# Two groups of tiles instead of three in the first sequence's first feed-forward, own tokens for the small loads, later strip and convolution matmuls

## The reference

```
mod = silu(c) @ w_mod + b_mod                      # 9 vectors: shift, scale, gate x 3
x   = x + 0.5 * g1 * FFN1(mod(rmsnorm(x)))         # width 2816, SwiGLU; also for the context
p   = mod(rmsnorm(x)) @ w_in                       # q k v, output gate, decays, conv input, merge gates
o   = bidirectional chunked gated linear attention(q, k, v, decays), starts from the context's state
z   = GLU(conv input);  y = silu(layernorm(depthwise conv of width 31 (z))) @ w_conv_out
x   = x + g2 * ((sigmoid(ga) * y + sigmoid(gb) * gla_output(o)) @ w_out)
x   = x + 0.5 * g3 * FFN2(mod(rmsnorm(x)));  out = rmsnorm(x)
```

## Time and profile before

| | us |
|---|---|
| median of 3 runs | 7281.48 (7276.81 to 7284.88) |
| profiled execution, its own time | 7291.05 |
| its span on the slowest core (core 2) | 7289.4 |
| spans of the eight cores | 7261.0 to 7289.4 |
| first matmul of FFN1, sequence 0 | 116.09 |
| groups 2 and 3 of FFN1 begin | 408.51, 588.41 |
| phase B of sequence 0 | 763.67 to 1258.29 |
| phase B of sequence 1 | 2555.00 to 3002.12 |
| last cast issued | 1005.91 |

### The profile page before, as it was taken

The page is one execution under the profiler, slowest core; times in us unless marked ns, Lnnn a source line. Parts: engine busy times, 40 slices in busy tenths (PEclk is TensorE's granted clock), DMA queues, the critical chain, the costliest instruction groups (busy, mean ns, idle before and its releaser), DMA issues.

```text
span 7289.4 us, 111871 instructions; the slowest of 8 cores (7261.0 to 7289.4 us)
## 1 busy us (share of the span) xinstructions
PE 6791.2 (93%) x38936; PEld 3421.5 (47%) x38936; DVE 3072.9 (42%) x5068; ACT 2844.4 (39%) x4883; POOL 607.2 (8%) x570
## 2 busy tenths in 40 slices
PE   4989887999999998899999998899999999879999
PEld 1435544444454455344445455444445445534444
DVE  2232455543324255544333345554432435554432
ACT  2132555322314266433233346533332436643321
POOL 0000222000000022100000012110000002210000
PEclk7999988999999999899999999999999999989999
DMA  8898865555545445655554544645553654555554
GB/s 181 200 229 184 154 118 129 176 186 182 176 135 196 162 94 98 171 163 175 180 176 155 180 140 95 139 157 187 182 175 123 196 168 108 102 138 170 188 184 148
DMA packets 466131, 1166.10 MB, mean 160 GB/s; under 512 B 54192, under 2 KB 202160, under 8 KB 460144
## 3 DMA queue, kind: packets, MB, share of 16 engines
q1 hardware_dynamic: 461840, 1103.03, 51.0%
q0 software_dynamic: 3744, 55.91, 5.8%
HBM read 1097.14 MB, written 173.08 MB: 174 GB/s over the span
## 4 chain that ended last, share of the span: by engine, by line
PE 82%; DMA 10%; SPq 4%; DVE 2%; issue 2%; ACT 1%; POOL 0%; DVEq 0%; ACTq 0%; POOLq 0%
PE pb L594 82%; DMA ZS_b<-z_s 4%; SPq L591 4%; DMA WU_f<-w_mod 2%; DMA z_s<-ZR_b 1%; DMA WH_f<-w_mod 1%; DVE NM_f L620 1%; DMA x_s<-X_f 0%; DMA WR_d<-wdn_s 0%; DMA WM_f<-w_mod 0%; DMA WR_g<-wg_s 0%; DMA z_s<-NM_b 0%; ACT L613 0%; ACT NM_f L613 0%; DVE R_f L623 0%
## 5 line engine op out<-in xcount | busy, mean ns | idle before, releaser
L594 PE MATMUL pb<-uF_b,WR_g 128*128 128x512 bf16 x11264 | 2474.1, 380 | 20.4 <-DMA WR_g<-wg_s 15.7
L613 ACT ACTIVATE EV_f<-pb 128x512 f32<-128x512 f32 (+1 forms) x1322 | 766.0, 582 | 2554.0 <-PE pb L594 2517.1
L594 PEld LDWEIGHTS pb<-uF_b,WR_g 128*128 128x128 bf16 x11264 | 1103.1, 98 | 1346.2 <-issue 48.4
L594 PE MATMUL pb<-U2T,WR_g 128*128 128x512 bf16 x6272 | 1448.9, 384 | 24.2 <-ACT EV_f L613 21.5
L594 PE MATMUL pb<-hF_b,WR_d 128*128 128x512 bf16 x5456 | 1195.5, 380 | 9.1 <-DMA WR_d<-wdn_s 9.1
L620 DVE TENSOR_TENSOR hF_b<-EV_f,pb 128x512 bf16<-128x512 f32 x682 | 468.1, 687 | 1503.1 <-PE pb L594 1420.8
L594 PEld LDWEIGHTS pb<-U2T,WR_g 128*128 128x128 bf16 x6272 | 614.5, 99 | 730.0 <-issue 82.6
L594 PEld LDWEIGHTS pb<-hF_b,WR_d 128*128 128x128 bf16 x5456 | 534.5, 98 | 654.3 <-issue 23.5
L613 ACT ACTIVATE NM_f<-X_f 128x512 f32<-128x512 f32 x504 | 305.8, 625 | 1029.9 <-DVE X_f L623 927.0
L623 DVE SCALAR_TENSOR_TENSOR X_f<-pb,SC,X_f 128x512 f32<-128x512 f32 x384 | 284.3, 750 | 934.9 <-PE pb L594 934.6
L620 DVE TENSOR_TENSOR NM_f<-NM_f 128x512 f32<-128x512 f32 (+1 forms) x672 | 471.4, 715 | 64.7 <-ACT NM_f L613 40.3
(11 more groups left out here) (141 smaller groups left out, 5545.9 us busy)
## 6 DMA issues: line engine op xcount, KB each, us to landing
WR_g<-wg_s SPq DMA_DIRECT2D x1130, 512.0 KB, 4.0
WR_d<-wdn_s SPq DMA_DIRECT2D x496, 352.0 KB, 3.2
ZS_b<-z_s SPq DMA_DIRECT2D x512, 131.0 KB, 6.1
wg_s<-wg POOLq DMA_DIRECT2D x84, 512.0 KB, 10.9
X_f<-x SPq DMA_DIRECT2D x64, 512.0 KB, 7.9
x_s<-X_f SPq DMA_DIRECT2D x64, 512.0 KB, 8.2
X_f<-x_s SPq DMA_DIRECT2D x64, 512.0 KB, 8.1
out<-X_f SPq DMA_DIRECT2D x64, 512.0 KB, 5.1
```

Of the source, the lines that this page charges most:

```text
L594: return (lambda e: e.matmul(out, lhsT, rhs, start=start, stop=stop), reads, writes)
L613: [(lambda e: e.activation(out, in_, func, **kw), reads, writes)], FUNC_SETS.get(func, 0))
```

## The change

It has five parts.

1. **Groups.** In sequence 0 the feed-forward has two groups, tiles 3, 2 and the context, then tiles 1 and 0. The context gets buffers of its own there (HC0, UC0, XC0), for which WU goes from two buffers to one. Tiles 1 and 0 both go through UTX, and U2T is free once three users are done (`u2_part`).
2. **Tokens.** The small loads (cst, vecs, gn, wa, dwc) and the three paddings of z_s have a token each instead of one together; the paddings are written in a task of their own (`pads`) after the seventh block of the second group; the four WM strips are four tasks; the first group's x and context are loaded ahead of the third strip.
3. **Later by plan.** `dma(..., late=)` adds to the time at which the planner expects a transfer: 6 us for WU and WH strips, 3 us for the loads ZS_b, in all sequences.
4. **Casts.** FFN1's 38 casts are paced as before. The 16 of QK and V come over the second group, the 24 of the merge over phase B's 16 weight blocks, and the 30 of FFN2 one for each weight load after them. Before, the 40 of QK, V and merge came over groups 2 and 3, and the 30 of FFN2 two for each load of phase B.
5. **Priority.** `prep_c`, `mean_c` and `ln_chunk` of tile 0 get 2 instead of 5 in every sequence.

```diff
-                    op.fin = self.dma_free + 1.4
+                    op.fin = self.dma_free + 1.4 + sets
...
-        WMU = mkpool("WU", 2, {"f": ([128, 8, 512], F32, 0)}, 1, [u2off])
+        WMU = mkpool("WU", 1, {"f": ([128, 8, 512], F32, 0)}, 1, [u2off])
+        HC0 = mkpool("hC0", 1, {"b": ([128, NJ, NCX], BF16, 0)}, NJ, [u2off + 16384])
+        UC0 = mkpool("uC0", 1, {"b": ([128, 8, NCX], BF16, 0)}, 8, [end_ac])
+        XC0 = mkpool("XC0", 1, {"f": ([128, 8, NCX], F32, 0)}, 8, [SB_END - SB_END % 64 - 8192])
...
-        t_zpad = T()
+        t_zpad = [T() for _ in range(3)]
+        t_cst, t_vec, t_gn, t_wa, t_dw = T(), T(), T(), T(), T()
...
-                elif n < n_ffn + n_mid:
-                    tick = len(refs_ffn(0)) - 2 + (n - n_ffn) * (len(refs_a(0)) - len(refs_ffn(0))) // n_mid
+                elif n < n_b:
+                    tick = lf - 2 + (n - n_ffn) * (la - lf) // (n_b - n_ffn)
+                elif n < n_c:
+                    tick = la + (n - n_b) * 16 // 24 - 2
                 else:
-                    tick = len(refs_a(0)) + (n - n_ffn - n_mid) // 2
+                    tick = la + 16 + n - n_c
...
-                g = [xs[:2]] + [[t] for t in xs[2:]]
-                if len(g) > 1:
-                    g[-1].append(NTT)
-                else:
-                    g.append([NTT])
-                return g
+                return [xs[:2] + [NTT]] + [xs[n:n + 2] for n in range(2, NTT, 2)]
...
-                    yield dma("sp", 134144, zs.h["b"][16 * r:16 * r + 16, :, :], zsrc(blk, gi, r), reads=rd, writes=[zs.ts[r]], cost=0.65)
+                    yield dma("sp", 134144, zs.h["b"][16 * r:16 * r + 16, :, :], zsrc(blk, gi, r), reads=rd, writes=[zs.ts[r]], cost=0.65, late=3.0)
...
-            M.spawn(mean_c(s, i, cv), 0, 5)
+            M.spawn(mean_c(s, i, cv), 0, 2 if i == 0 else 5)
...
-                M.spawn(ln_chunk(s, i, c, cv, mean, va), 0, 5)
+                M.spawn(ln_chunk(s, i, c, cv, mean, va), 0, 2 if i == 0 else 5)
...
+                elif part == 2 and len(gr) > 1:
+                    yield wait("A", 0, gr[1][0], "h", (ch - 12) * 3)
...
+        def pads():
+            yield wait("A", 0, a_groups(0)[-1][0], "h", 6)
...
-            M.spawn(mod_task(range(0, 4), 0), 0, 0)
+            for ch in range(4):
+                M.spawn(mod_task([ch], 0), 0, ch // 2 * 2)
...
-            for dst, src in ((vecs[:], vecs_d), (gn[:], gn_d)):
-                yield dma("sp", 65536, dst, src, writes=[t_c])
+            yield dma("sp", 81920, vecs[:], vecs_d, writes=[t_vec])
+            yield dma("sp", 4096, gn[:], gn_d, writes=[t_gn])
...
-                M.spawn(prep_c(s, 0), 0, 5)
+                M.spawn(prep_c(s, 0), 0, 2)
```

More of the change, by code:

```diff
@@ L587, in build, with dma @@
         dsems = {e: [es.enter_context(nc.semaphore(f"d_{e}{i}")) for i in range(NDMASEM[e])] for e in ENGS}
-        def dma(q, nb, out, in_, reads=(), writes=(), cost=0.45, **kw):
+        def dma(q, nb, out, in_, reads=(), writes=(), cost=0.45, late=0, **kw):
             return ("op", q, cost if q != "pool" else 1.0,
-                    [(lambda e: e.dma_start(out=out, in_=in_, **kw), reads, writes)], nb, 0)
+                    [(lambda e: e.dma_start(out=out, in_=in_, **kw), reads, writes)], nb, late)
         def mmi(out, lhsT, rhs, start, stop, reads, writes):
@@ L778, in prep_a @@
             isx, W, col, tok0 = ainfo(s, ti)
-            late = (s, ti) == late_tile
+            late = (s, ti) in late_tiles
             if late:
                 yield wait("sc", 1)
-            X = yield acq(UTX if late else XP if isx else XCP)
+            X = yield acq(UTX if late else XP if isx else XCS[s])
             xf = X.h["f"]
@@ L785, in prep_a @@
             sm = yield from norm_sum(lambda c: xf[:, c, :W], X.ts, W)
+            if s == 0:
+                yield wait("const")
             rs = yield from rstd_of(sm, W)
@@ L800, in prep_a, with u2_part @@
                 M.flag("X", "A", s, ti)
+        def u2_part():
+            info["u2n"] = info.get("u2n", 0) + 1
+            if info["u2n"] == len(late_tiles) + 1:
+                u2_free()
         def u2_free():
             ops = []
-            for b in WMP.bufs[2:] + WMU.bufs + UTX.bufs:
+            for b in WMP.bufs[2:] + WMU.bufs + UTX.bufs + HC0.bufs:
                 ops += b.hist
@@ L848, in ffn @@
         def ffn(mem, which, after=None):
-            for (key, W, col, hb, up) in mem:
-                yield wait("u", *key)
             for j in range(NJ):
+                if j == 0:
+                    yield wait("u", *mem[0][0])
                 wb = yield from wnext(ref_g((G_GU1, G_GU2)[which] + j))
@@ L854, in ffn @@
                 for (key, W, col, hb, up) in mem:
+                    if j == 0:
+                        yield wait("u", *key)
                     u = info[key][1]
@@ L939, in phase_a @@
                 mem = []
-                hc = None
-                hp = None
+                extra = []
                 for n2, ti in enumerate(g):
                     isx, W, col, tok0 = ainfo(s, ti)
+                    hc = hb
                     if not isx:
-                        yield wait("u", "A", s, ti)
-                        hp = HCP
-                        hc = yield acq(hp)
+                        hp = HCS[s]
                     elif n2 == 1 and g[0] < NTT:
                         hp = HP2
+                    else:
+                        hp = None
+                    if hp is not None:
+                        if not isx and s > 0:
+                            yield wait("u", "A", s, ti)
                         hc = yield acq(hp)
-                    mem.append((("A", s, ti), W, col, hb if isx and hp is not HP2 else hc, UP if isx else UCP))
+                        extra.append((hp, hc))
+                    mem.append((("A", s, ti), W, col, hc, UP if isx else UCS[s]))
                 yield from ffn(mem, 0)
-                if hc is not None:
+                for hp, hc in extra:
                     hp.rel(hc)
-                if s == 0 and n == 0 and late_tile is None:
+                if s == 0 and n == 0:
                     yield wait("sc", 1)
-                    u2_free()
+                    u2_part()
                 for ti in g:
@@ L1026, in conv_task @@
                 zs = yield acq(ZS)
-                rd = [t_z[blk][i2] for i2 in near] + [t_zpad]
+                rd = [t_z[blk][i2] for i2 in near] + t_zpad
                 for r in range(8):
-                    yield dma("sp", 134144, zs.h["b"][16 * r:16 * r + 16, :, :], zsrc(blk, gi, r), reads=rd, writes=[zs.ts[r]], cost=0.65)
+                    yield dma("sp", 134144, zs.h["b"][16 * r:16 * r + 16, :, :], zsrc(blk, gi, r), reads=rd, writes=[zs.ts[r]], cost=0.65, late=3.0)
                 for e in range(2):
@@ L1054, in gates @@
         def gates(s, h, d, hl):
-            order = border[1:-1] + [border[0], border[-1]] if s == 0 and h == 0 else border
+            order = border
             pool = GD[d]
@@ L1622, in mod_task @@
                 PS.rel(pt)
-                if ch == 3:
-                    M.flag("sc", 0)
+                if ch < 4:
+                    info["sc0"] = info.get("sc0", 0) + 1
+                    if info["sc0"] == 4:
+                        M.flag("sc", 0)
                 elif ch == 5:
```

57 lines of the change are left out of this document (31 added, 26 removed).

## The result

The changed kernel takes 0.9863 of the time of before, 95% interval 0.9834 to 0.9892: some 100 us less than 7281 us. Two of its six executions, 7174.4 us (the profiled one) and 7188.4 us, ran with a granted clock of 0.97 or 0.98 on all cores; in the others the four cores of one half of the chip, or all eight, had a lower one and took 7866 to 8357 us, and such executions and cores are left out in all that follows. Over the eight cores of the profiled executions the median span fell from 7272.7 to 7160.4 us, 112 us. The forecast was 157 us.

What follows compares the result with a forecast made beforehand. PE, busy 93% of 7289.4 us, was taken as the bound, leaving its waits and half-clock time; -38 - 83 - 3 + 4 - 9 + 20 + 3 x (-7 - 9) = -157 us gave 7125 us, range 7085 to 7160, ends 7065 and 7205.

Steps and rivals of the forecast that it cites:

- signs of being wrong: Phase B longer in sequences 1 to 3, or the merge of sequence 0 losing nothing or more than 50 us.
- Casts, +20: First merge and its feed-forward: 21 FFN2 casts moved there fill DMA and delay weights, +20 us (0 to +48).
- The rival of a starving merge: First merge: late casts make FFN2's weights hold PE too, 70 us more, about 7195 us; chance 15%.
- Feed-forward, -83: Sequence 0's feed-forward: two groups save 38 weight loads, 565 us against 647.6, -83 us (-95 to -60).
- WU waits: First feed-forward group: with one WU buffer, strips come late and PE waits some 15 us, a sign to look for.
- Start, -38: Before the first feed-forward matmul: no waits for small loads, FFN1 starts at 78 us, -38 us (-52 to -28).
- Phase B, end, -7: End of phase B, sequences 1 to 3: both averages ahead of work, 11 us idle instead of 18, -7 us each.
- convolution, -9: Phase B, each sequence: lateness moves ZS_b matmuls back and shortens their waits, -9 us (0 to -25).
- The 4 to 9 us wait ahead of s1's average: Phase B of sequence 1: sign that PE would wait 4 to 9 us for a POOL addition there.
- the waits for ZS_b: Phase B's convolution: sign that PE's waits for ZS_b would be near 115 us, from 154.3.
- Phase B of sequence 0, -8: Phase B of sequence 0: -3 us at its end, -9 convolution, +4 strip matmuls moved in from phase A.
- The rule on queues: First merge: DMA engines alternate between queues packet by packet; half left to loads would just fit, sum about 15 us lower.

Runs made afterwards that it cites:

- e1: Changed kernel with the old pacing of the casts (40 over the second group, FFN2's 30 two per phase B load): 7198.5 us.
- b4: Kernel before with only the two groups, their buffers and the later strips, casts by the old rule: 7260.5 to 7266.3 us, against 7291.0 before.
- b1: Kernel before with only the new pacing of the casts, still three groups: 7311.7 us, against 7291.0 before on this chip.
- b2: Kernel before with only the tokens, the order of the first loads and the later paddings: 7255.7 us, 35 less than before on its chip.
- e4: Changed kernel with priority 5 again for tile 0's prep_c, mean_c and ln_chunk: spans of 7144.2 to 7178.5 us on cores 4 to 7.
- b3: Kernel before with only the 3 us of lateness for ZS_b loads: 7222.5 to 7234.7 us on cores 4 to 7, against 7253.4 to 7265.7 before.
- e3: Changed kernel without the planner's 3 us of lateness for the ZS_b loads: 7230.0 to 7244.7 us.
- c3: Changed kernel with FFN2's casts at one per two loads, tile 0's norm at priority 5, and ZS_b lateness 6 us: 7135.7 and 7145.5 us.
- c1: Changed kernel with FFN2's casts at one per two weight loads and tile 0's norm at priority 5: 7121.2, 7128.4 and 7167.8 us.

## Why the prediction was right, and which terms were not

**Direction and range** held, some 7180 us against 7125 in 7065 to 7205; the narrower 7085 to 7160 did not. The difference in the sum, 112 us instead of 157, is nearly all one term, the casts. Of the prediction's own signs of being wrong one came true: the merge of sequence 0 lost more than 50 us.

**Casts, +20, measured +61.** The place was right, and that the loads wait for casts; the size lay beyond even the 48 us that I allowed. I priced the weights' waits and took seven buffers as a cushion, and left out that loads without a cushion, x and OG_b of the second merge, stand in the same queue. e1 shows that all 61 us are the casts'. The rival of a starving merge, with FFN2's weights late because their casts are, did not come true: from 1295 to 1380 us PE is busy for 85.00 of 85 us at a clock of 1.00.

**Feed-forward, -83, measured -87**, partly by luck. I counted 38 casts for FFN1, and the text on the change says so too; there are 30 (22 blocks and 8, not 16, of down). The first group's DMA need is then 274 - 44 = 230 us of 292, 0.79, and 0.77 was measured; WU waits were 1.3 us, not some 15. And I gave all of the term to the saved loads. Measured alone, the groups with the later strips bring 53 us (b4) and the pacing 57 (b1); both with the earlier start, which costs phase A 7 (b2), bring 87. The pacing's part is hardly a gain of the kernel: it comes back in merge 0 (b1) or nearly so (e1).

**Start, -38, measured -30.** The chain that ended last has one of the last x loads there, issued at 14.1 us:

```profile
14.05 44.35 DMA X_f<-x
```

The matmuls of the third and fourth strip stand behind the three averages of the norms, so x counts as well. But the strips were hardly earlier: the fourth landed at 74.1 us, not 69, and its matmuls began at 75.6. The queues up to the first feed-forward matmul:

```profile
q1 hardware_dynamic: 4288, 16.45, 64.2%
q0 software_dynamic: 465, 3.47, 31.0%
```

All together that is 240 GB/s, but the loads moved at 16.45 MB / (0.642 x 83 us) = 309 GB/s of their own time, so the 297 that I reckoned with held, and the casts at 135. What I had left out is the four weight blocks that SP issues from 37 to 55 us, 2.1 MB or some 7 us of the engines: up to 74.1 us the queue had moved 16.0 MB, not 13.9.

**Phase B, end, -7, measured 0** (e4), and **convolution, -9, measured -17 to -24** (b3): the sum of -16 a sequence was right, but not its parts. Undone one at a time in the changed kernel the priority is worth 0 and the lateness 6 to 10; each on its own would give 6 to 11 and 17 to 24. I followed the wait from the matmul that held it, and added the two where one chain carries both. The 4 to 9 us wait ahead of s1's average that I named as a sign is not there, and the waits for ZS_b are 87.6 us, not 115.

**Phase B of sequence 0, -8, measured -3.** Small in sum and not small in its parts: casts -12 (b1), groups +20 (b4), ZS_b late +10 before the change and -40 in it (e3, b3), priority +15 (e4). Why the same lateness works in opposite directions there stays open; the planner's order of this phase differs in every kernel.

**The rule on queues.** By the Trainium skill ("DMA: Bandwidth & Descriptors", Queues, rings and completion order) casts and loads take turns on each engine, packet by packet. From this I worked out that the loads would have half the engines, that the merge's loads would just fit and the sum be 15 us lower. The trace agrees with the turns: the casts landed after 11.0 and 13.9 us whatever SP had waiting. It does not give the half: a cast's packet takes about ten times as long as a load's (2.0 us against 0.2), and with a turn each the loads had 31.2% of the engines, the casts 67.0%. The numbers for it stand in the earlier trace rows already: 5.8% for 3744 packets, 51.0% for 461840, so 1.8 us against 0.13. The time that my reading gave was wrong by 56 us. How many of them are due to this and how many to the missing cushion, no run tells.

## What to carry to other kernels

Where a background transfer is moved from a full stretch to another, price it in both by what it delays there, and look for loads with no ring of buffers ahead of them: 20 casts cost 61 us in a merge with a cushion of seven weight buffers, and the longest wait, 27.4 us, was for one OG_b. Price the share that each queue gets by the time of its packets, which the profile's queue lines give. When the order of an in-order engine comes from a planner, its estimate of a latency is a tuning knob of its own: 3 us on one kind of load gave 17 to 24 us in each later sequence (b3), 6 us gave less (c3). And sum an in-order engine's waits along the chain that they belong to, not by the instruction that holds them, or one chain is won twice.

## What was not expected of the hardware

Two queues that were both busy did not share the engines evenly. With casts always under way (1150 to 1250 us) they had 67.0% of the engines' time for 8.28 MB, and SP's loads 31.2% for 8.16 MB: a cast's packet took about 2.0 us and a load's 0.22.

And a transfer of 256 KB took 53.9 us to land at a DMA share of 0.91, and 21.9 us at 0.89 in c1: the share alone did not tell how long a load waits. The split did: the loads' queue had 37.3% of the engines in the one window and 48.8% in the other.
